# Gates of the second attention and the last feed-forward stage multiplied into the weights

## The reference, cut

```python
def second_block(x, c, w_ada, b_ada, ...):
    sc = jax.nn.silu(c)
    for i in range(DEPTH):                       # DEPTH = 2
        mod = sc @ w_ada[i] + b_ada[i]           # 1024 -> 6 * 1024
        sh_m, sc_m, g_m, sh_f, sc_f, g_f = jnp.split(mod, 6, axis=-1)
        h = modulate(x, norm_mix[i], sh_m, sc_m)
        if i % N_MIXERS == 0:
            y = moba_attention(h, w_qkv[j], w_o[j], q_gain[j], k_gain[j])
        else:
            y = short_conv(h, w_in[j], conv_w[j], w_out[j])
        x = x + g_m[:, None, :] * y
        h = modulate(x, norm_ffn[i], sh_f, sc_f)
        x = x + g_f[:, None, :] * swiglu(h, w_gate_up[i], w_down[i])
    return x
```

## Time and profile before

| | us |
|---|---|
| median of 3 runs | 1260.29 (1259.63 to 1262.46) |
| the profiled execution | 1260.91 |
| its span, first to last instruction | 1259.1 |
| TensorE busy in the span | 1231.9 (98%) |
| VectorE busy | 945.2 (75%) |
| ScalarE busy | 719.2 (57%) |
| mean rate of the DMAs | 209 GB/s |

### The profile page before, as it was taken

One profiled execution on the slowest core, in us unless ns is written; L12 is line 12 of the kernel. 1 busy time (PEld: TensorE's weight loads), 2 busy tenths in 40 slices (PEclk: granted clock), 3 DMA queues, 4 the chain that ended last, 5 costly groups with the idle time before them and its releaser, 6 DMA issues.

```text
span 1259.1 us, 23514 instructions
## 1 busy us (share of the span) xinstructions
PE 1231.9 (98%) x9891; PEld 1149.3 (91%) x9891; DVE 945.2 (75%) x1279; ACT 719.2 (57%) x1048; POOL 16.4 (1%) x28
## 2 busy tenths in 40 slices
PE   6999999999999999999999999999999999999998
PEld 6989899999899879999988998999998998999997
DVE  5887379888768777999977567799976666677453
ACT  6833477656664667666667556644455544644432
POOL 0011000000000000000000000000000000000000
PEclk9999999999999999999999999999999999999999
DMA  9450287875657156789763534899965356675540
GB/s 323 165 201 4 69 268 234 267 249 203 218 201 268 68 184 218 239 271 310 251 221 107 192 135 134 285 349 364 334 240 201 135 202 200 231 245 194 201 167 34
DMA packets 163875, 263.78 MB, mean 209 GB/s; under 512 B 5869, under 2 KB 98233, under 8 KB 163770
## 3 DMA queue, kind: packets, MB, share of 16 engines
q1 hardware_dynamic: 160586, 259.54, 60.2%
q10 hardware_dynamic: 3184, 2.73, 0.7%
HBM read 261.17 MB, written 1.05 MB: 208 GB/s over the span
## 4 chain that ended last, share of the span: by engine, by line
PE 92%; DVE 3%; ACT 2%; issue 2%; DMA 1%; SPq 0%; ACTq 0%; DVEq 0%
PE ps L1087 25%; PE ps L1058 16%; PE ps L1060 15%; PE ps L1059 15%; PE ps L827 2%; PE ps L828 2%; PE ps L829 2%; PE ps L2334 2%; PE ps L1073 2%; PE ps L1075 1%; PE ps L1074 1%; PE ps L807 1%; DMA arena<-in_w_ada_dram 1%; DVE wlo L603 1%; DMA ring<-in_ev_w_in_dram 1%
## 5 line engine op out<-in xcount | busy, mean ns | idle before, releaser
L603 DVE TENSOR_TENSOR wlo<-ring,whi 128x2048 fp32r<-128x2048 f32 x194 | 443.1, 2287 | 98.5 <-ACT whi L597 98.5
L1058 PE MATMUL ps<-ghi,whi 128*128 128x256 f32 x1600 | 448.7, 280 | 0.0
L1059 PE MATMUL ps<-glo,whi 128*128 128x256 f32 x1600 | 447.0, 279 | 0.0
L1060 PE MATMUL ps<-ghi,wlo 128*128 128x256 f32 x1600 | 446.9, 279 | 0.0
L597 ACT ACTIVATE whi<-ring 128x2048 fp32r<-128x2048 f32 x194 | 370.6, 1914 | 82.1 <-PE ps L1087 48.2
L1058 PEld LDWEIGHTS ps<-ghi,whi 128*128 128x128 f32 x1600 | 300.4, 188 | 1.2
L1059 PEld LDWEIGHTS ps<-glo,whi 128*128 128x128 f32 x1600 | 299.8, 187 | 1.2
L1060 PEld LDWEIGHTS ps<-ghi,wlo 128*128 128x128 f32 x1600 | 300.7, 188 | 0.0
L1087 PE MATMUL ps<-whi,yhi 128*128 128x512 f32 x480 | 159.4, 396 | 0.7 <-DVE ylo L1935 0.7
L1087 PE MATMUL ps<-wlo,yhi 128*128 128x512 f32 x480 | 156.8, 390 | 0.0
L1087 PE MATMUL ps<-whi,ylo 128*128 128x512 f32 x480 | 156.7, 390 | 0.0
(11 more groups left out here) (306 smaller groups left out, 1574.4 us busy)
## 6 DMA issues: line engine op xcount, KB each, us to landing
arena<-in_w_ada_dram SPq DMA_DIRECT2D x48, 1024.0 KB, 6.1
ring<-in_ff_w_up_dram SPq DMA_DIRECT2D x44, 1024.0 KB, 7.6
ring<-in_w_gate_up_dram SPq DMA_DIRECT2D x44, 1024.0 KB, 7.2
ring<-in_ff_w_down_dram SPq DMA_DIRECT2D x10, 2048.0 KB, 7.9
ring<-in_w_down_dram SPq DMA_DIRECT2D x10, 2048.0 KB, 8.0
ring<-in_od_w_qkv_dram SPq DMA_DIRECT2D x6, 2048.0 KB, 8.6
ring<-in_w_qkv_dram SPq DMA_DIRECT2D x6, 2048.0 KB, 8.0
ring<-in_w_in_dram SPq DMA_DIRECT2D x6, 2048.0 KB, 7.9
```

Of the source, the lines that this page charges most:

```text
L603: e.tensor_tensor(shaped(WLO[i % NB], k), v, shaped(WHI[i % NB], k).bitcast(F32), ALU.subtract).then_inc(S["w_lo"], 1)
L1058: e.matmul(o, wh, h[0][:, k, :], start=k == 0, stop=False)
L1059: e.matmul(o, wh, h[1][:, k, :], start=False, stop=False)
L1060: x = e.matmul(o, wl, h[0][:, k, :], start=False, stop=k == NK - 1)
```

## The change

Three things change.

First, for `o2` and `down3` the gate is multiplied into the weights in the ring: VectorE multiplies each half of 128 x 2048 in place with the gate, repeated for the two rows of columns that the half holds (`gate_half`), 4 halves of `o2` and 11 of `down3`. The product of half i + 1 stands behind the wlo of half i, and ScalarE's whi of a gated half waits for that product and no longer for the landing. For k = 5 and k = 8 the sums are then added to x as they are.

Second, the two blocks of the last gate (four steps) move in `ADA_AT` from tiles 5, 7, 9 and 11 of feed-forward 3 to tiles 2, 3, 4 and 5 of `cin`, with their four DMAs, their parts and their sums (which are then at tiles 7 and 9 of `cin`).

Third, a memset early in the kernel counts on another semaphore.

```diff
--- before.py
+++ after.py
@@ -113,10 +113,12 @@
     ("qkv", [("tile", i) for i in (2, 3, 4, 5)]),
     ("ffn1", [("tile", i) for i in (5, 7, 9, 11, 13, 15, 17)] + [("rows", i) for i in (0, 4, 6, 8, 12)]),
     ("ffn2", [("tile", i) for i in range(3, 17)] + [("rows", i) for i in range(0, 12, 2)]),
-    ("cin", []),
-    ("ffn3", [("tile", i) for i in (5, 7, 9, 11)]),
+    ("cin", [("tile", i) for i in (2, 3, 4, 5)]),
+    ("ffn3", []),
 ]
 MOD_Q = {0: 0, 1: 1, 3: 2, 4: 3}
+
+GATED = {"o2": (0, 0), "down3": (1, 1)}
 
 
 
@@ -588,10 +590,24 @@
                 first, self.made = self.made, max(self.made, end)
                 return range(first, end)
 
+        gated_halves = [i for i, (n, _, _, _) in enumerate(halves) if chunks[n][0][0] in GATED]
+
+        def gate_half(e, i):
+
+            n, v, _, _ = halves[i]
+            l, f = GATED[chunks[n][0][0]]
+            for h in range(2):
+                e.wait_ge(*read_out(("ada", 12 * l + 6 * f + 4 + h)))
+            e.wait_ge(S[f"ring{n % NS}"], landed[n])
+            e.tensor_tensor(c3(v, 2), c3(v, 2), rep(GB[l][f], 2), ALU.mult).then_inc(S["w_gated"], 1)
+
         def split_hi(e, which):
             for i in which:
                 n, v, k, _ = halves[i]
-                e.wait_ge(S[f"ring{n % NS}"], landed[n])
+                if i in gated_halves:
+                    e.wait_ge(S["w_gated"], gated_halves.index(i) + 1)
+                else:
+                    e.wait_ge(S[f"ring{n % NS}"], landed[n])
                 if i >= NB:
                     e.wait_ge(S["w_used"], i - NB + 1)
                 e.activation(shaped(WHI[i % NB], k), v, ACT.Copy).then_inc(S["w_hi"], 1)
@@ -602,6 +618,8 @@
                 e.wait_ge(S["w_hi"], i + 1)
                 e.tensor_tensor(shaped(WLO[i % NB], k), v, shaped(WHI[i % NB], k).bitcast(F32),
                                 ALU.subtract).then_inc(S["w_lo"], 1)
+                if i + 1 in gated_halves:
+                    gate_half(e, i + 1)
 
         def first_piece(x, p):
             return x[:, 1024 * p:1024 * p + 1024]
@@ -763,14 +781,14 @@
         SHIFT = [None] * 4 + [modc[:, l, 2 * q, :] for l, q in TWO]
 
         SUM_OF = [None, "ev_out", "down0", "od_out", "down1", "o2", "down2", "out2", "down3"]
-        GATE_OF = [None] * 5 + [GB[l][f] for l, f in TWO]
+        GATE_OF = [None] * 6 + [GB[0][1], GB[1][0], None]
 
         def x_ready(k, n, h):
 
             if k == 0:
                 return S[f"x{n}"], 16
             if GATE_OF[k] is not None:
-                return S["x_gated"], 4 * (k - 5) + 2 * n + h + 1
+                return S["x_gated"], 4 * (k - 6) + 2 * n + h + 1
             return read_out(("sum", SUM_OF[k], n, h))
 
 
@@ -1157,7 +1175,7 @@
 
             dve_residual(e, k, 0)
             dve_scaled(e, k, 0, dve_rstd(e, k, 0))
-            if k > 4:
+            if GATE_OF[k] is not None:
                 dve_gated(e, k, 1, 0)
                 dve_turned(e, k, 0)
                 dve_added(e, k, 1, 0)
@@ -1772,15 +1790,14 @@
             split_lo(e, w.go())
             mixed(2)
             e.wait_ge(S["consts_in"], 16)
-            e.memset(SS[:, :, :, 0:1], 0.0).then_inc(S["ss_zero"], 1)
+            e.memset(SS[:, :, :, 0:1], 0.0).then_inc(S["scanned"], 1)
             for j in range(4):
                 e.wait_ge(*read_out(("sg", 0, j // 2)))
                 for n in range(2):
                     x = e.tensor_tensor_scan(SS[:, j, n, 1:129], ones, W0[:, j, 128 * n:128 * n + 128], 0.0,
                                              ALU.mult, ALU.add)
             x.then_inc(S["scanned"], 1)
-            e.wait_ge(S["ss_zero"], 1)
-            e.wait_ge(S["scanned"], 1)
+            e.wait_ge(S["scanned"], 2)
             mid = SS[:, :, :, 64]
             e.tensor_scalar(c3(KS, 4), mid, KAPPA, None, ALU.mult).then_inc(S["ss_mid"], 1)
             e.tensor_scalar(c3(NKS, 4), mid, -KAPPA, None, ALU.mult).then_inc(S["ss_mid"], 1)
```

## The result

The changed kernel takes 1265.15 us (median of 6 executions, 1263.71 to 1265.99), the kernel before 1260.36 in the same comparison (6 executions). The ratio is 1.0034, 95% interval 1.0024 to 1.0044: slower by 4.8 us. The forecast was 1265.4, range 1262.0 to 1267.8. So the direction is settled, and the three medians put its size at 2.9 to 4.8. Their intervals are 3.0 to 5.5, 1.8 to 5.0 and 1.6 to 4.3 us; they overlap, so the three don't contradict one another.

What follows compares the result with a forecast made beforehand. TensorE, busy 1231.9 of 1259.1 us, was taken as the bound. Stall 4.3, clock 1.5 and end -0.7 gave +5.1 us: 1266.0 for the profiled execution, 1265.4 as median, range 1262.0 to 1267.8.

Steps and rivals of the forecast that it cites:

- The bound and the lead: Convolution input stage: VectorE keeps pace with nothing to spare but its lead, 7.7 and 8.0 us at tiles 8 and 9.
- The steps' price and the wlo starts: Tiles 2 to 5: steps of 2.77 or 3.02 us, subtraction 0.60; wlo starts near 1002.0, 1010.7, 1019.5 and 1027.9.
- The DMAs of the steps: Convolution input stage: the steps' four DMAs arrive in time and add no delay.
- Where TensorE waits: Convolution input stage: TensorE waits 1.0 us before tile 8 and 3.4 in one piece before the second sum.
- The stall of 4.3: Convolution input stage: tile 9 starts 4.3 us late, beyond 0.91 for the two moved sums.
- The bound of 4.8: Convolution input stage: the stall costs at most 4.8 us, 12.2 less the lead of 8.0 plus 0.6.
- The clock's 1.5: Behind the 3.4 us wait before tile 9: TensorE's clock falls to its lower level, adding 1.5 us, or 0.
- the first rival: Convolution input stage: the stall comes but the clock stays up, 4.3 - 0.7 = +3.6, 1263.9 us; chance 0.28.
- The ring products: Attention output and last down projection: 15 VectorE products of 2.29 us, cost 0; upper bound about 2 us late.
- The norm: Norm behind the attention output: dropping its four products gains 0, at most the 2.0 us of two waits.
- The lead is enough: Rival, convolution input stage: lead and whi waits take the 12.2 us of steps, only 0.7 left, 1259.6; chance 0.14.
- The end: End of the kernel: the last product goes and the last addition starts 0.73 us sooner, -0.7.

Runs made afterwards that it cites:

- e3: The changed kernel with the four steps in tiles 2, 3, 6 and 7 of cin instead of 2 to 5: 1262.39 us against 1260.67 before.
- r5: The changed kernel itself, measured again in a later group: 1264.12 us against 1261.22 for the kernel before, ratio 1.0027.
- e4: The changed kernel with the subtraction of a finished block ahead of its tile's step in cin, not behind it: 1266.51 us against 1260.67 before.
- r10: The changed kernel with the subtraction ahead of the step, as in e4, run again beside r9: 1267.99 us against 1261.49 before.
- r7: The changed kernel with a second VectorE operation of equal size ahead of each of the 15 ring products: 1285.81 us against 1261.22 before.
- r9: The changed kernel itself once more, on the same chip as r10: 1264.40 us against 1261.49 for the kernel before, ratio 1.0023.
- r6: The changed kernel with the four steps in tiles 0, 1, 6 and 7 of cin: 1259.18 us against 1261.22 before, ratio 0.9985.
- e2: The kernel before with only the attention output's weights gated in the ring, steps left in the last feed-forward stage: 1259.93 us against 1260.67.
- r8: r6 with the last addition between the two low parts in the norm behind the attention output: 1258.14 us against 1261.22 before, ratio 0.9977.
- e1: The kernel before with only the four steps moved to tiles 2 to 5 of cin, gate products left in place: 1267.62 us against 1260.67.

## Why the prediction was right, point by point

- **The bound and the lead.** Right. That TensorE has a lead of 7.7 and 8.0 us in tiles 8 and 9 is borne out from both sides: delays of 9.2 and 12.2 stalled it, a delay of 6.4 (e3) did not.
- **The steps' price and the wlo starts.** Right. Forecast 1002.0, 1010.7, 1019.5, 1027.9. In r5 the norm ahead came 1.43 us earlier than in the earlier trace rows, and the starts are 1000.59, 1009.29, 1018.05 and 1026.47: with the 1.43 added, the forecast to the hundredth or two. The profiled execution first shown has 1002.55, 1011.25, 1020.01 and 1028.43 with a norm that came 0.91 later, so 0.4 earlier than forecast in each (these 0.4 are the pace: its run-in took 10.81 and not 11.19).
- **The DMAs of the steps.** Right: no step waits for its data, where the attention's had waited 1.82.
- **Where TensorE waits.** The step that failed: "TensorE comes there at 1020.35 + 0.45, the 0.45 being the first of two sums" took the first sum as free. The sum needs the first subtraction, which VectorE makes behind the third step, from 1016.23, and TensorE stood there for 1.82 us. The wait of 1.0 before tile 8 didn't come, since that delay was already paid; by the prediction's own words ("It is wrong if tile 8 starts without a wait") this part of it was wrong. It came in e4 and r10, where the first sum had nothing to wait for; and the 3.4 in one piece became 2.42 (or 0.87, with the clock's loss ahead of it). I had looked up when the second subtraction is made and not when the first is.
- **The stall of 4.3.** Right within 0.4. The traces of this order show 4.34, 4.33, 4.72 and 4.74 (and r7 4.33), which at one pace is 4.7 in all five, because VectorE and ScalarE set when tile 9 can start, however TensorE's idle time ahead of it is cut. That the first trace read 4.34 is the pace and not the sum's exactness. The 0.4 more than forecast are what a wait costs beside its own length: in r5 the matmul ahead of the first sum starts at 1013.00 and the one behind it at 1015.62, which is 2.62 us for a wait of 1.81, two matmuls of 0.23 and the usual 0.12 from one start to the next, so 0.24 are over, and as much at the second sum; 4.23 + 0.48 = 4.7. The bound of 4.8 held.
- **The clock's 1.5.** Wrong as a term of this sum. It was priced behind one piece of 3.4 us; that piece did not exist, and a fall behind the first piece is absorbed by the second. Where the piece does exist (e4, r10) the term is larger than 1.5: 7.39 and 7.40 less 4.72 are 2.7 in both, since the clock stays low for 6.8 us and not for the 3.0 read from the first attention. So the mechanism of the changed kernel is that of the first rival, the stall without the clock: 4.3 - 0.7 = 3.6 as forecast, 4.7 - 0.7 = 4.0 as measured, and both lie in the intervals of all three comparisons. The forecast's +5.1 lies in the first interval alone. That 1265.4 met the 1265.15 of the first group to 0.3 us was luck: a term that the traces don't bear out, and a median 0.8 to 1.2 us further from the kernel before than the stall explains. Whether that distance is more than chance the overlapping intervals leave open. The profiled execution of this group has a fall of the clock that the profiled kernel before doesn't have (0.60 in 72 to 76 us), long ahead of the moved steps and the products, and is 0.91 us behind at the norm ahead of the stage (981.02 against 980.11). The memset, at 39.0 us, is the only changed instruction ahead of that fall. r9 and r6 show the fall too; the other seven with the same memset (e2, e3, e4, r5, r7, r8, r10) don't.
- **The ring products.** Price right (2.28 us each, 15 of them), net cost 0 right (e2; and no wait in the gated stages). The bound above, "about 2 us late" for twice the price, was wrong by a factor of ten for the kernel and of three to four for the attention alone (6.2 us of waits, 8.2 with the clock behind them), since it moved one row by one product instead of adding four products along a chain.
- **The norm.** 0, right: e2. That the addition "stands behind that low part again" was right too; r8 shows that the 0.7 us could be had by moving it.
- **A rival's sum.** "The lead is enough" doesn't come out even on its own condition: 7.7 us of lead and the waits of 0.3, 0.3, 1.1 and 1.1 are 10.5, and the delay at half 9 is 12.2, so about 2 us of stall would have been left. Its 0.14 was too much.
- **The end.** -0.73, right. In e1, with the product, the last addition starts at 1261.56, 0.72 behind the product; in the changed kernel only an addition follows the last matmul.

The Trainium skill, TensorE: Matmul & The Clock Gate, Part 1: The HAM clock gate, says that idleness brings the clock back to its lower level, and that the same kernel sees different numbers of slow matmuls from run to run. The traces agree with both: the clock fell in both traces with a wait of 3.2 or 3.4 us, and behind the same 1.8 us in two profiled executions of the changed kernel but not in the third. By the first rule alone the sum had the 1.5; it needs beside it what stands behind the fall.

## What to carry to other kernels

A step moved onto an engine that keeps pace with nothing to spare is paid in full beyond the lead, and the debt is handed on past the stage until the engine is idle ahead of its own work: look for the next place where someone waits for it (here the norm, one stage later), and put the step where the engine is idle ahead of the tight stretch. The length of such a stall shows only when executions of the same matmul pace are set beside each other; here the pace alone moved it by 0.4. An engine's idle share isn't cover when that engine sits in a loop of three with every link dependent; add up the loop and compare it with the consumer's pace. Before adding a price for a slower clock behind a stall, ask whether another wait for the same late engine follows, since that wait gives the loss back, up to its own length.

## What was not expected of the hardware

- The clock fell behind a wait of 1.8 us in two executions of one kernel (and in r7), and not in a third (nor in e1, with the same order); a wait of 2.4 us in that third and in e1 was followed by no fall. How long it stayed low differed too. Behind the 1.8 it was one stretch of 3.5 us at 0.54. With the waits of 3.2 and 3.4 us (e4, r10) it was about 6.8 us: in r10 the granted clock was 0.73 in 1028 to 1033 and 0.58 in 1033 to 1038, and it fell while TensorE was still waiting. With the 7.1 us in r7 it was low from 1264.2 to 1274.3.
- The same matmuls of one kernel ran at two paces with the granted clock at 1.00 in each. In the run-in one matmul of 128x256 follows the other by 0.118 us in the kernel before and by 0.113 in the changed kernel's first profile. It took 11.19 or 11.20 us in five traces (the kernel before, e1, e2, r5, r10) and 10.80 to 10.82 in seven (the changed kernel's first profile, e3, e4, r6, r7, r8, r9); r5 and r9 are the same kernel. The difference is 0.38 of the -0.56 in the stage of r6 and r8. Its cause stays open.
